# First attention of a two-block transformer kernel: two of eight key chunks of the probabilities are kept whole and meet V in fp32 products

## What is computed

```python
def blocked_gqa(q, k, v):
    q = q * jnp.asarray(1.0 / math.sqrt(HEAD_DIM), q.dtype)
    qb = q.reshape(B, nb, Q_BLOCK, N_KV_HEADS, Q_PER_KV, HEAD_DIM).transpose(1, 0, 2, 3, 4, 5)
    def one_block(qblk):
        s = jnp.einsum('bqkgd,bskd->bkgqs', qblk, k).astype(jnp.float32)
        p = jax.nn.softmax(s, axis=-1).astype(v.dtype)
        return jnp.einsum('bkgqs,bskd->bqkgd', p, v)
    o = lax.map(one_block, qb)
```

## Time and profile before

| | |
|---|---|
| median of 3 runs | 2482.29 us (2481.96 to 2482.37) |
| profiled execution, its own time | 2479.31 us |
| its span, first to last instruction | 2477.5 us |
| PE busy | 2344.5 us, 95% |
| DVE busy | 1117.5 us, 45% |
| ACT busy | 775.9 us, 31% |
| POOL busy | 860.2 us, 35% |
| granted TensorE clock, mean | 0.982 |

### The profile page before, as it was taken

The page is one execution under the profiler, slowest core; times in us unless marked ns, Lnnn a source line. Parts: engine busy times, 40 slices in busy tenths (PEclk is TensorE's granted clock), DMA queues, the critical chain, the costliest instruction groups (busy, mean ns, idle before and its releaser), DMA issues.

```text
span 2477.5 us, 30786 instructions
## 1 busy us (share of the span) xinstructions
PE 2344.5 (95%) x11310; PEld 1925.1 (78%) x11310; DVE 1117.5 (45%) x1381; ACT 775.9 (31%) x1096; POOL 860.2 (35%) x851
## 2 busy tenths in 40 slices
PE   4897888999999999999999999999999999999997
PEld 3676777777888888888777888887778888888886
DVE  7958888478641344124463334353211122222324
ACT  3216777123320222023424445462122111112220
POOL 1345554225423333323233323232223334333331
PEclk9998999999999999999999999999999999999999
DMA  7311000623211111111131111102011111111132
GB/s 303 111 38 43 17 17 10 255 102 131 89 51 51 43 51 51 43 60 51 38 115 63 39 53 51 39 30 83 30 36 45 51 51 51 51 47 38 51 127 77
DMA packets 48318, 166.02 MB, mean 67 GB/s; under 512 B 4480, under 2 KB 6272, under 8 KB 48128
## 3 DMA queue, kind: packets, MB, share of 16 engines
q1 hardware_dynamic: 48256, 165.19, 19.4%
HBM read 156.79 MB, written 8.39 MB: 67 GB/s over the span
## 4 chain that ended last, share of the span: by engine, by line
PE 80%; DVE 9%; issue 4%; ACT 4%; POOL 1%; DMA 1%; SPq 0%; DVEq 0%; ACTq 0%; POOLq 0%
PE acc L747 62%; PE turn L972 6%; PE bank L1036 3%; DVE ADA L1656 1%; PE bank L1014 1%; PE acc L960 1%; DVE HL L1636 1%; DVE acc L1812 1%; PE turn L641 1%; PE bank L849 1%; ACT EX L1259 1%; PE acc L725 1%; DMA ADA<-in_ada 1%; PE bank L1111 1%; PE bank L1108 1%
## 5 line engine op out<-in xcount | busy, mean ns | idle before, releaser
L747 PE MATMUL acc<-HH,WH 128*128 128x512 f32 x1600 | 498.3, 393 | 16.0 <-POOL WL L541 15.1
L747 PE MATMUL acc<-HL,WH 128*128 128x512 f32 x1600 | 495.0, 391 | 0.0
L747 PE MATMUL acc<-HH,WL 128*128 128x512 f32 x1600 | 494.1, 390 | 0.0
L538 POOL TENSOR_TENSOR WH<-WF,CON 128x16 fp32r<-128x16 f32 x186 | 49.5, 266 | 1224.1 <-PE acc L747 1009.4
L541 POOL TENSOR_TENSOR WL<-WF,WH 128x1024 fp32r<-128x1024 f32 (+2 forms) x186 | 441.3, 2372 | 15.5
L747 PEld LDWEIGHTS acc<-HH,WH 128*128 128x128 f32 x1600 | 301.0, 189 | 82.3 <-POOL WL L541 13.0
L747 PEld LDWEIGHTS acc<-HL,WH 128*128 128x128 f32 x1600 | 301.9, 189 | 63.3
L747 PEld LDWEIGHTS acc<-HH,WL 128*128 128x128 f32 x1600 | 301.6, 189 | 63.1
L539 POOL TENSOR_SCALAR WH<-WF 128x1008 fp32r<-128x1008 f32 (+2 forms) x186 | 192.5, 1035 | 0.0
L1942 DVE SCALAR_TENSOR_TENSOR CV<-EV,VEC,CV 128x1023 f32<-128x1023 f32 x44 | 99.1, 2251 | 204.0 <-ACT CV L1335 203.3
L1870 DVE SCALAR_TENSOR_TENSOR XT<-acc,MOD,XT 128x1024 f32 (+1 forms) x34 | 43.6, 1284 | 233.0 <-PE acc L747 233.0
(11 more groups left out here) (374 smaller groups left out, 4104.2 us busy)
## 6 DMA issues: line engine op xcount, KB each, us to landing
WF<-in_w SPq DMA_DIRECT2D x150, 512.0 KB, 3.3
ADA<-in_ada SPq DMA_DIRECT2D x15, 1024.0 KB, 14.8
BIAS<-in_bias SPq DMA_DIRECT2D x16, 576.0 KB, 3.8
XT<-in_xT SPq DMA_DIRECT2D x16, 512.0 KB, 10.0
ADA<-in_ada SPq DMA_DIRECT2D x4, 2048.0 KB, 11.8
ADA<-in_ada SPq DMA_DIRECT2D x3, 2560.0 KB, 9.2
WF<-in_w SPq DMA_DIRECT2D x24, 256.0 KB, 2.6
ADA<-in_ada SPq DMA_DIRECT2D x8, 512.0 KB, 3.3
```

Of the source, the lines that this page charges most:

```text
L538: pool.tensor_tensor(h[:, 0:FEW], f[:, 0:FEW], zero.to_broadcast([P, FEW]), ALU.add).then_inc(w_hi, 1)
L747: last = pe.matmul(acc[:, slot, HALF * c:HALF * c + HALF], w[slot][:, k, :], x[:, k, HALF * c:HALF * c + HALF], start=(k == 0 and w is WH ...
```

## The change

Of the eight key chunks of a unit, numbers 6 and 7 are no longer split. ACT copies their turned probabilities as fp32 into a new tile `PTF` (first, 128x256), and chunks 4 and 5 into `PTH` (128x256). DVE takes remainders of chunks 0 to 5 alone: 128x512 and 128x256. `values` goes over six chunks with two fp32r products each; in front of chunk 4 it has two new products, one per whole chunk, with fp32 operands: `VF` (V of those chunks, 64 stationary columns) times `PTF` (256 columns), into the lower half of `bank6`. V's own split covers six chunks, and `VF` is a copy of the rest. `PTF` and `VF` lie where the parts of `PTH` and `PTL` for chunks 6 and 7 lay. No semaphore is added or counts otherwise.

```diff
+        PTF = at("PTF", 44, [P, 2, 4, P])
+        VF = at("VF", 60, [P, 2, NKV, HD])
...
-                    for k in range(TT):
+                    for k in range(6):
                         if k % 4 == 0:
                             pe.wait_ge(ptl_ready, now + (2 + k // 4 + 1))
+                        if k == 4:
+                            for i in range(2):
+                                pe.matmul(bank6[0:HD, P * c:P * c + 2 * P], VF[:, i, b % 2, :], PTF[:, i, c:c + 2, :],
+                                          start=False, stop=False)
                         for x in (PTH, PTL):
                             mm = pe.matmul(bank6[:, P * c:P * c + 2 * P], VTOK[:, k, b % 2, :], x[:, k, c:c + 2, :],
-                                           start=(k == 0 and x is PTH), stop=(k == TT - 1 and x is PTL))
+                                           start=(k == 0 and x is PTH), stop=(k == 5 and x is PTL))
...
-                        act.activation(PTH[:, 4 * h:4 * h + 4, u % 4, :],
-                                       turns[(2 * u + h) % 3].rearrange("p (k q) -> p k q", q=P), ACT.Copy
-                                       ).then_inc(pth_ready, 1)
+                        x = turns[(2 * u + h) % 3].rearrange("p (k q) -> p k q", q=P)
+                        n = 4 - 2 * h
+                        if h == 1:
+                            act.activation(PTF[:, :, u % 4, :], x[:, 2:4, :], ACT.Copy)
+                        act.activation(PTH[:, 4 * h:4 * h + n, u % 4, :], x[:, 0:n, :], ACT.Copy).then_inc(pth_ready, 1)
...
-            act.activation(vdst[:, :, 0:HD], vt, ACT.Copy).then_inc(vh_ready, 1)
+            act.activation(VF[:, :, :, :], turn[:, 6 * P:].rearrange("p (t v d) -> p t v d", t=2, d=HD), ACT.Copy)
+            act.activation(vdst[:, 0:12, 0:HD], vt[:, 0:12, :], ACT.Copy).then_inc(vh_ready, 1)
...
-            dve.tensor_tensor(vdst[:, :, HD:P], vt, vdst[:, :, 0:HD].bitcast(F32), ALU.subtract).then_inc(vl_ready, 1)
+            dve.tensor_tensor(vdst[:, 0:12, HD:P], vt[:, 0:12, :], vdst[:, 0:12, 0:HD].bitcast(F32), ALU.subtract
+                              ).then_inc(vl_ready, 1)
...
-                        dve.tensor_tensor(PTL[:, 4 * h:4 * h + 4, u % 4, :],
-                                          turns[(2 * u + h) % 3].rearrange("p (k q) -> p k q", q=P),
-                                          PTH[:, 4 * h:4 * h + 4, u % 4, :].bitcast(F32), ALU.subtract).then_inc(ptl_ready, 1)
+                        ks = slice(4 * h, 4 + 2 * h)
+                        dve.tensor_tensor(PTL[:, ks, u % 4, :],
+                                          turns[(2 * u + h) % 3].rearrange("p (k q) -> p k q", q=P)[:, 0:4 - 2 * h, :],
+                                          PTH[:, ks, u % 4, :].bitcast(F32), ALU.subtract).then_inc(ptl_ready, 1)
```

## The result

The changed kernel takes 2494.65 us (median of five executions, 2494.01 to 2496.95), the kernel before 2482.29 (2481.24 to 2483.38): a ratio of 1.0053, 95% interval 1.0039 to 1.0067. It is slower by half a per cent. The profiled execution took 2494.65 us with a span of 2492.8, where the earlier trace rows come from one of 2479.31 with 2477.5. The forecast was 2494.3.

A forecast was written before the change was run, and what follows sets the result against it. No engine is full in the first attention, so the order of waits decides: 3 x 2.85 + 3.5 - 0.3 + 0.2 = 12.0 us makes 2491.3 profiled, plus 3.0 for the median: 2494.3 us; range 2486.0 to 2497.5.

The forecast's parts named there:

- The cost of V: TensorE, first attention: each product with V grows 0.72 us: -0.48 records dropped, +0.86 fp32 records, +0.34 width change.
- The slacks: How long finished scores lie before VectorE's largest-value pass can use them: 0, 0.84, 0.07, 0.36, 0, 0.83 us.
- V(3): V(u) is the product with V of units u-1 and u, issued in unit u+1; this one ends 0.72 late, slack 0.
- VectorE's saving: Second remainder pass 0.27 us shorter, 64 times, 17 us busy time; counts only in units 5 and 13.
- the split copies: ScalarE's 512-column copy becomes two of 256: 0.07 us each, at most 0.17, on the path in units 1 and 2.
- rival D: Split copies don't overlap, ScalarE leads in units 1, 2, 9, 10: 2.7 for 0.9, 2496 us; 0.70 together with forecast.
- the sum: First attention's total: 3 x 2.85 + 3.5 - 0.3 (V's split) + 0.2 (first iteration's copies) = 12.0 us.
- Rival A: TensorE's width change costs nothing, or slack is larger than read: +2 to +7 us; chance 0.18.
- v = 0.38: Lower bound for each V's growth, width costing nothing: 1.1 us per iteration, 4.7 in all, 2487.0 us.
- the end of the iteration: After V(u) with u = 15, which has no slack, all engines move together to the next V(3): +2.85 us per iteration.
- rival C: Late scores also delay exponential and POOL; TensorE's clock drops more often at iteration ends: 2498 us or above; chance 0.06.
- the 3.0: Whole kernel: the median of three runs exceeded the profiled execution by 3.0 us; the same difference was put on the forecast.

The follow-up runs named there:

- the old products: Changed kernel with sixteen fp32r products in V again, chunks 4 and 5 entered twice, 6 and 7 missing; split copy and shorter remainder kept: 2480.59 us, ratio 0.9996.
- the kernel with 128 columns: Changed kernel with VF padded by 64 zero columns, so the fp32 products have 128 stationary columns and write both halves of bank6: 2486.39 us, ratio 1.0021.
- the filled kernel: Changed kernel with twelve extra unread fp32 products of the identity in TensorE's idle time in unit 1 of each iteration: 2495.86 us, ratio 1.0055.
- the products alone: Kernel before with only two fp32 products of the rounded parts in V for chunks 6 and 7, their remainders unused: 2493.27 us, ratio 1.0052.

## Why the prediction was right

**The cost of V** was worked out from two stages far behind the attention and held in each part: 0.216 per fp32 record, 0.34 for the width, 0.72 in all (2.71 us against 1.99).

**The slacks.** The start of each V in the second iteration, read from PE's timeline, and its delay over that of V(3):

| V | before | after | delay, predicted | delay, measured |
|---|---|---|---|---|
| (3) | 286.57 | 290.35 | 0 | 0 |
| (5) | 293.06 | 297.56 | 0.72 | 0.72 |
| (7) | 299.51 | 303.88 | 0.60 | 0.59 |
| (9) | 306.10 | 311.09 | 1.25 | 1.21 |
| (11) | 312.18 | 317.40 | 1.45 | 1.44 |
| (13) | 318.68 | 324.61 | 2.17 | 2.15 |
| (15) | 324.71 | 330.51 | 2.06 | 2.02 |
| (3), next | 341.54 | 349.02 | 2.85 | 3.70 |

Up to V(15) each step is met to 0.05 us. The largest-value passes that wait, changed kernel, timeline of DVE:
```profile
294.30 1.29 DVE L1822 TENSOR_SCALAR_CACHE_REDUCE acc<-acc,RSN 128x1024 f32<-128x1024 f32 x1 [0.69 <-PE acc L836]
...
301.51 1.29 DVE L1822 TENSOR_SCALAR_CACHE_REDUCE acc<-acc,RSN 128x1024 f32<-128x1024 f32 x1 [0.19 <-PE acc L836]
...
307.82 1.29 DVE L1822 TENSOR_SCALAR_CACHE_REDUCE acc<-acc,RSN 128x1024 f32<-128x1024 f32 x1 [0.68 <-PE acc L836]
...
315.03 1.29 DVE L1822 TENSOR_SCALAR_CACHE_REDUCE acc<-acc,RSN 128x1024 f32<-128x1024 f32 x1 [0.34 <-PE acc L836]
...
321.35 1.29 DVE L1822 TENSOR_SCALAR_CACHE_REDUCE acc<-acc,RSN 128x1024 f32<-128x1024 f32 x1 [0.69 <-PE acc L836]
```
They follow V(3), V(5), V(7), V(9) and V(11), whose slacks were read as 0, 0.84, 0.07, 0.36 and 0 us: the waits are long where there was little slack and short where there was much. In the fourth iteration the delays were 0.71, 0.62, 1.32, 2.05, 2.75 and 2.62, where 0.72, 0.6, 1.25, 1.97, 2.7 and 2.8 were predicted.

**VectorE's saving and the split copies** count for nothing together that the medians can tell: 0.9996 (0.9987 to 1.0005). The argument was that the saving counts in two units of an iteration; the trace of the old products has these 0.4 to 0.5 us. In rival D the price of the split copies is off: it takes 0.9 out of the sum where the sum holds 0.07 x 3 + 0.2 = 0.4, so its time would be 2496.6 in place of 2496. Rival A is out for the change itself, since the width does cost 0.33; its time, 2487.0 for v = 0.38, is what the kernel with 128 columns took (2486.39).

**The step that was mis-sized** is the end of the iteration. The prediction gave the stage from V(15) to V(3) 0.79 us and priced a drop of the clock at 0.14 (rival C), by the one drop in the earlier trace rows. The stage grew by 2.83, 1.68 and 1.45, and a drop with a mean clock of 0.91 cost 0.9 us. What the 0.14 left out is that the price depends on what falls into the drop. Behind V(1) the largest-value pass waits for its scores, in the first and the second drop of the changed kernel and in the one of the kernel before:
```profile
287.98 1.29 DVE L1822 TENSOR_SCALAR_CACHE_REDUCE acc<-acc,RSN 128x1024 f32<-128x1024 f32 x1 [1.33 <-PE acc L836]
346.65 1.29 DVE L1822 TENSOR_SCALAR_CACHE_REDUCE acc<-acc,RSN 128x1024 f32<-128x1024 f32 x1 [0.78 <-PE acc L836]
394.27 1.29 DVE L1812 TENSOR_SCALAR_CACHE_REDUCE acc<-acc,RSN 128x1024 f32<-128x1024 f32 x1 [0.29 <-PE acc L834]
```
In the third drop of the changed kernel no such wait is there, and V(1) ran at full clock. The transposes behind the idle time did not. Here they are for that drop, for the one of the kernel before, and for the first and the third of the kernel with the old products:
```profile
397.11 1.11 PE L870 MATMUL bank<-CON,EX 128*128 128x128 f32 x4 [3.23 <-POOL EX L573]
...
401.37 0.36 PE L855 MATMUL bank<-PTH,VTOK 128*128 128x256 f32 x1
```
```profile
386.88 0.66 PE L864 MATMUL bank<-CON,EX 128*128 128x128 f32 x4 [3.24 <-POOL EX L571]
```
```profile
276.32 1.11 PE L871 MATMUL bank<-CON,EX 128*128 128x128 f32 x4 [3.24 <-POOL EX L573]
...
387.69 0.66 PE L871 MATMUL bank<-CON,EX 128*128 128x128 f32 x4 [3.24 <-POOL EX L573]
```
ScalarE's copies wait for these transposes, and the exponential and the next largest-value pass stand behind them. In the third drop that pass came 4.25 us behind the one before it (396.72 to 400.97), in the filled kernel 3.44 (338.90 to 342.34). The kernel with the old products has a V of the old length and pays both prices: its stage took 17.76 us where the transposes ran slow and 17.00 where they didn't, with a mean clock of 0.90 in both. So a dear drop needs no longer V. That the longer V adds to the price in the first two drops, by the waits of 1.33 and 0.78 against 0.29, is argued and was not tested alone.

So what rival C describes did happen beside the forecast's chain, in the profiled execution, with 3.9 us. Since the drops came with the old products too, the runs don't show that the change caused these 3.9.

**The number itself** was closer than its parts deserve. For the profiled execution 2491.3 us was forecast, and it took 2494.65: 3.3 more. The output projection starts 14.3 us later than before (452.59 against 438.30). Without the 3.9 for drops that is 10.4, where the sum has 12.0; about half of the difference is that V(1) starts 1.0 us earlier (223.55 against 224.56), where 0.3 was forecast. Behind that point the span grew by another 1.0, for which the sum has nothing. So 3.9 - 1.6 + 1.0 = 3.3. The median then hid it: the profiled execution before was 3.0 us under its median, that of the changed kernel was its median, and the prediction had carried the 3.0 over. That the two cancel is luck. The kernel with the products alone, without a drop, is the cleaner witness for the chain: 11.5 us at the same point.

## What to carry to other kernels

A unit of work that an engine isn't full with can still be on the path: read, for each hand-over, how long the result lay before it was used, and send the growth through that list step by step. Removing work from the engine with the most busy time gives next to nothing where its next step waits for another. Before a wait is moved away by reordering, list everyone who waits for the end of the moved work; here there were two, and each order served one. And a short product with another number of stationary columns between others costs as much as several products.

## What the runs showed of the hardware

The 64-column group between 128-column ones costs 0.33 us per visit (2.71 against 2.38), nearly as much as three fp32r products of 256 columns.

A fall of TensorE's granted clock has no fixed price, and what falls into it matters. With a mean clock of 0.90 the same stage of one kernel took 17.76 us where the transposes that others wait for ran slow (four in 1.11 us) and 17.00 where they ran at full speed (0.66). In the kernel before such a fall cost 0.14 us (16.97 against 16.83), in the changed one 0.9 (18.51 against 17.61).

Executions of the kernel before spread from 2475.7 to 2484.6 us over two comparisons, more than the change of some experiments. One thing that differs from one execution to the next is when a weight load of the gated FFN lands, issued behind loads of the modulation's matrix. The chain of waits of the kernel with the old products shows it:
```profile
618.49 9.59 DMA WF<-in_w
```
POOL waited 11.6 us for it, and 8.4 in the profile of the kernel before; from the output projection's start to the fifth copy to `GH` on ScalarE it took 227.4 us and 224.8. The kernel with the filled idle time had it as well (11.7, and 227.6), the changed kernel didn't (6.6, and 226.4). How much of the spread it makes, and what decides it in an execution, was not tried.
